# Three shared tiles instead of two in the score search of a sparse-attention block (Trainium2, one core)

## What is computed

```python
act = jax.nn.relu(jnp.einsum('bqhd,bsd->bqsh', qib, ki) * idx_scale)
score = jnp.einsum('bqsh,bqh->bqs', act, wib)
score = jnp.where(key_pos[None, None, :] < chunk_end[None, :, None], score, -jnp.inf)
_, sel = lax.top_k(score, topk)
```

## Time and profile before

| what | value |
|---|---|
| time, median of 3 runs | 1994.21 us (1988.74 to 1998.3) |
| time of the profiled execution | 1992.56 us |
| span of the profiled execution, first to last instruction | 1991.1 us |
| TensorE busy | 1716.8 us, 86% of the span |
| VectorE busy | 1114.5 us, 56% |
| ScalarE busy | 765.3 us, 38% |
| GpSimd busy | 379.1 us, 19% |
| mean granted TensorE clock | 0.945 of full speed |

### The profile page before, as it was taken

The page is one execution under the profiler, slowest core; times in us unless marked ns, Lnnn a source line. Parts: engine busy times, 40 slices in busy tenths (PEclk is TensorE's granted clock), DMA queues, the critical chain, the costliest instruction groups (busy, mean ns, idle before and its releaser), DMA issues. The chain is left out here.

```text
span 1991.1 us, 34351 instructions
## 1 busy us (share of the span) xinstructions
PE 1716.8 (86%) x14024; PEld 1387.2 (70%) x14024; DVE 1114.5 (56%) x2131; ACT 765.3 (38%) x1192; POOL 379.1 (19%) x337
## 2 busy tenths in 40 slices
PE   1999885699749967889769899999999999999796
PEld 0777663288637756778647688888888888888584
DVE  5266654789956644767535555444446544444463
ACT  4153432577445533333123333222233332223441
POOL 2232320032122210122313421000012100001442
PEclk9999987799969989999788899999999999999898
DMA  2116551122111023120072222222232332333122
GB/s 107 60 54 185 168 162 47 48 75 96 64 44 54 12 82 140 47 89 15 13 269 64 71 95 90 99 101 96 96 95 95 127 95 95 95 96 95 43 85 95
DMA packets 91959, 177.14 MB, mean 89 GB/s; under 512 B 7392, under 2 KB 51456, under 8 KB 91808
## 3 DMA queue, kind: packets, MB, share of 16 engines
q1 hardware_dynamic: 62688, 160.33, 24.1%
q10 hardware_dynamic: 29120, 14.68, 2.6%
HBM read 138.81 MB, written 36.18 MB: 88 GB/s over the span
## 5 line engine op out<-in xcount | busy, mean ns | idle before, releaser
L781 PE MATMUL acc<-h_hi,w_hi 128*128 128x512 f32 x768 | 309.3, 403 | 23.2 <-DVE w_lo L845 19.5
L782 PE MATMUL acc<-h_lo,w_hi 128*128 128x512 f32 x768 | 303.8, 396 | 0.0
L783 PE MATMUL acc<-h_hi,w_lo 128*128 128x512 f32 x768 | 303.4, 395 | 0.0
L685 ACT ACTIVATE w_hi<-w_raw 128x1024 fp32r<-128x1024 f32 x160 | 168.4, 1052 | 155.2 <-DMA w_raw<-w_ffn 144.3
L845 DVE TENSOR_TENSOR w_lo<-w_raw,w_hi 128x1024 fp32r<-128x1024 f32 x160 | 203.3, 1271 | 1.3 <-ACT w_hi L685 1.3
L781 PE MATMUL acc<-ffn_hi_lo,w_hi 128*128 128x512 f32 x512 | 200.2, 391 | 0.0
L782 PE MATMUL acc<-ffn_hi_lo,w_hi 128*128 128x512 f32 x512 | 199.3, 389 | 0.0
L783 PE MATMUL acc<-ffn_hi_lo,w_lo 128*128 128x512 f32 x512 | 199.3, 389 | 0.0
L781 PEld LDWEIGHTS acc<-h_hi,w_hi 128*128 128x128 f32 x768 | 147.2, 192 | 58.4 <-DVE w_lo L845 21.9
L504 POOL TENSOR_TENSOR post_squares_total<-post_squares_total,post_squares 128x512 f32<-128x512 f32 x42 | 64.6, 1539 | 570.9 <-ACT post_squares L497 570.1
L782 PEld LDWEIGHTS acc<-h_lo,w_hi 128*128 128x128 f32 x768 | 147.6, 192 | 32.2 <-issue 1.9
(11 more groups left out here) (304 smaller groups left out, 3587.7 us busy)
## 6 DMA issues: line engine op xcount, KB each, us to landing
w_raw<-w_ffn SPq DMA_DIRECT2D x128, 512.0 KB, 3.4
rwkv_factors<-factors_then_masks ACTq DMA_DIRECT2D x28, 512.0 KB, 6.3
factors<-rwkv_factors SPq DMA_DIRECT2D x32, 448.0 KB, 6.9
w_in_first_raw<-w_in SPq DMA_DIRECT2D x19, 512.0 KB, 3.8
w_raw<-w_out SPq DMA_DIRECT2D x16, 512.0 KB, 3.6
w_raw<-w_gate SPq DMA_DIRECT2D x16, 512.0 KB, 3.5
w_in_raw<-w_in SPq DMA_DIRECT2D x12, 512.0 KB, 3.9
x_in<-xT SPq DMA_DIRECT2D x8, 512.0 KB, 6.5
```

Of the source, the lines that this page charges most:

```text
L685: act.activation(wh[:, g % RING, :], w_raw[:, g % RING, :], ACT.Copy).then_inc(rounded, 1)
L781: pe.matmul(out, w_hi, a_hi, start=first, stop=False)
L782: pe.matmul(out, w_hi, a_lo, start=False, stop=False)
L783: return pe.matmul(out, w_lo, a_hi, start=False, stop=last)
```

## The change

`shared` gets a third tile, TILES - 3 = 5, which has 768 keys. ScalarE now counts tiles 5, 6 and 7 (768 + 896 + 1024 = 2688 keys a bit, before 1920), and VectorE tiles 2, 3 and 4 (384 + 512 + 640 = 1536 keys a bit, before 2304). The slice `both`, on which L1889 and the small instructions after the search work, covers three columns instead of two, as do the four small tiles of that part. VectorE waits for three counts of ScalarE a bit. The count of L1905 runs for three tiles instead of two.

```diff
         PER_BLOCK, BITS = 3, 32
-        shared = (TILES - 2, TILES - 1)
-        both = slice(shared[0] - FIRST, shared[1] - FIRST + 1)
+        shared = (TILES - 3, TILES - 2, TILES - 1)
+        both = slice(shared[0] - FIRST, shared[-1] - FIRST + 1)
         signs = {t: junk[t] for t in shared}
         limit, minus, reached = [ctx.sb(n, [P, T], F32) for n in ("limit", "minus_threshold", "reached")]
-        flip, low, high, carry = [ctx.sb(n, [P, 2], U32) for n in ("order_flip", "low_half", "high_half", "carry")]
+        flip, low, high, carry = [ctx.sb(n, [P, len(shared)], U32) for n in ("order_flip", "low_half", "high_half", "carry")]
...
                 link(last)
-                dve.wait_ge(counted, n * 2 + 2)
+                dve.wait_ge(counted, (n + 1) * len(shared))
                 link(dve.tensor_tensor(reached[:, :], count[:, :], limit[:, :], ALU.is_ge))
```

## The result

The changed kernel takes 2013.84 us in the median of 12 runs (2003.03 to 2021.65); the kernel before took 1996.49 us in the median of 12 runs beside it. The ratio is 1.0081, with a 95% interval of 1.0060 to 1.0102: slower by 0.8%. The profiled execution took 2009.5 us, with a span of 2008.0 us (1991.1 before) and a mean granted clock of 0.944.

The account below looks back on a forecast made before the run. VectorE's masks, starting where the search ends, end the stage; VectorE led the search, and ScalarE would lead after the change. Terms sum to +19.7 us: 2012.3 from the profiled execution, 2013.9 from the median; forecast 2013, range 2006 to 2021.

Parts of the forecast that it names:

- first block: Search's start up to ScalarE's copy of projection block 0: that copy comes 0.8 us later (0.4 to 1.1).
- copy 0 to copy 1: Between ScalarE's copies of projection blocks 0 and 1: 10.99 us becomes 13.10, so +2.11 us.
- copies 1 to 5, with values: ScalarE's copies of projection blocks 1 to 5, with turned values: each block 11.88 us becomes 14.01, +8.52 us together.
- Who leads: Search: a bit takes ScalarE 4.07 us, above VectorE's 3.81, so ScalarE leads in every bit.
- The price of the count: ScalarE's added count of 768 keys in each bit: 0.94 us, range 0.89 to 1.04.
- The way back: From ScalarE's last count through VectorE's comparison, predicated copies and new threshold to ScalarE's next start: 0.87 us a bit.
- The trip: ScalarE's copy and rounding for TensorE once a block: 1.85 us to the first count, 2.76 with turned values.
- The cover: Work costed at nothing: TensorE's projection gets gaps of 2 to 3 us a block but stays off the path.
- ScalarE's waits swallow the counts: Rival: ScalarE's idle time in the search absorbs the added counts, about 1990 us, not slower; chance 3%.
- The clock: Rival: new gaps make TensorE's clock fall, whole projection blocks at 1.2 GHz, near 2070 us; chance 3%.
- The stretch by GpSimd in the middle of the search: Rival: GpSimd's remainder stretches VectorE's return by 1.06 us in each of ten blocks, 2023 us; chance 4%.
- the change doesn't do what it says: Rival: for instance, the bound is a common one that neither tile assignment touches; no change, chance 2%.

Follow-up runs that it names:

- E1: The kernel before with a spare ScalarE count of 768 keys added in each bit, VectorE shedding nothing: 2011.72 us, ratio 1.0068.
- E5: The changed kernel with the smallest tile as the third, so ScalarE counts tiles 2, 6 and 7: ratio 1.0038 against the kernel before.
- E3: The changed kernel with ScalarE's third count over only 384 of the 768 keys: ratio 1.0028 against the kernel before.
- E2: The changed kernel with the third tile's count left out, so neither engine counts it: 1992.5 us, ratio 0.9986 against the kernel before.
- E4: The changed kernel with the copies of projection blocks 0 to 10 moved from ScalarE to VectorE: ratio 1.0032 against the kernel before.
- E6: The changed kernel with the copy of the best count run after the new threshold has gone out: ratio 1.0071 against the kernel before.
- E7: The kernel before with the copy of the best count run after the new threshold has gone out: ratio 0.9997.

## Why the prediction was right

The forecast was 2013 us in a range of 2006 to 2021, slower with 94%. Measured were 2013.84 us, slower with its whole interval. By its own steps, in the stage:

| term | forecast | measured |
|---|---|---|
| first block | +0.8 | 12.48 - 11.90 = +0.6 |
| copy 0 to copy 1 | +2.11 | 12.88 - 10.99 = +1.9 |
| copies 1 to 5, with values | +8.52 | 4 x (13.79 - 11.88) = +7.6 |
| copies 5 to 9 | +6.64 | 4 x (12.88 - 11.44) = +5.8 |
| copy 9 to the last comparison | +0.65 | 9.25 - 8.58 = +0.7 |
| L1905, third tile | +0.94 | +0.96 |
| together | +19.7 | +17.5 |

*Who leads.* Right: ScalarE leads in all 32 bits (the wait rows after), and E1 and E5 show that VectorE's share is worth nothing then.

*The price of the count.* Right: 0.932 us for 0.94. For 384 keys E3 measured 0.612, where the line through the two rows of before would have given 0.65 (0.94 less three times 0.097). An estimate by the rule of the Trainium skill, "ScalarE: Activation LUTs", section "What ACT_TABLE_LOAD costs", is 0.92 us for 768 keys; the trace lies between that and 0.94. The same estimate is 0.60 us for 384 keys, nearer to what E3 measured than the line is.

*The way back.* This is the term that was mis-sized. The forecast took 0.87 us from the earlier trace rows, where the bit follows the trip. There VectorE's comparison took 0.25 us instead of 0.17. In the changed kernel the way back has 0.79 us, outside the first block and the last bit. E2 has both in one block: 0.87 us before the bit at 477.43, the first after the rounding, and 0.79 before the one at 480.49. What ran beside the first of them on GpSimd:

```profile
474.48 2.41 POOL L380 TENSOR_TENSOR w_in_lo<-w_in_raw,w_in_hi 128x1024 fp32r<-128x1024 f32 x1 [8.46 <-ACT w_in_hi L376]
```

It ends at 476.89, and VectorE's comparison, from 476.66, took 0.25 us. Behind the first block this holds in all nine traces: the comparison takes 0.25 us or a little more where it begins while a remainder still runs, and 0.17 where none does. So the forecast's 0.87 us belongs to a bit that meets the remainder. The forecast had said itself that the remainder would no longer meet VectorE's small instructions, but it kept the price of a row in which it did. No run took the remainder away, so that it is the cause rests on this coincidence. A bit came out at 3.98 us instead of 4.07: about 0.1 us in each of the 18 inner bits of nine blocks is 1.6 to 1.8 of the 2.2 us between forecast and stage. The rest is 0.2 in the first block and 0.02 a block in the third bit's counts. The last bit's way back was 0.94 us although no remainder ran then; why, the runs don't show.

*The trip.* Right: 1.85 us without values and 2.76 with them, as in the earlier trace rows. A block without values grew by 1.44 us (12.88 - 11.44), and its two inner bits by only 0.17 each; the rest is the trip and the third bit's counts, which VectorE's counts no longer hide. E4 takes the copy out and gets 9.1 us back.

*The cover.* Right: TensorE's gaps came at block 6, and its last block was long done before the masks were. They were 1.7 to 2.2 us, for 2 to 3 forecast.

*The rivals.* That ScalarE's waits swallow the counts: E3 and E5 show that 0.61 us is already too much; the 0.39 us of the forecast was not tried. The clock: it stayed at the full level through all gaps. The stretch by GpSimd in the middle of the search: VectorE's comparison took 0.17 us in every bit but the second, where it took 0.59 beside GpSimd's work on `bias_rows`. That the change doesn't do what it says: the new shape stands 32 times in ScalarE's groups.

*The number.* That 2013 came within 1 us of 2013.84 is in part luck. The sum was 2.2 us too high, and the median that it was added to, 1994.21 of three runs, was 2.3 us below the 1996.49 of the twelve; the two errors cancel. The upper bound by the higher starting point is 1994.21 + 22.9 = 2017.1 and not 2016.8, which changes nothing in the range.

## What to carry to other kernels

Where two engines work through rounds that end in a common decision, the idle time of the one that follows is not room: subtract the way back of the round and the trips that it makes for others, and only the rest can take work. Here 0.67 us seemed free in one bit. Over a block it is less: in E3 a block without its three counts took 11.93 - 3 x 0.61 = 10.10 us, so 11.44 - 10.10 = 1.34 us was room for three, 0.45 each; with values it is 11.88 - (12.83 - 3 x 0.61) = 0.88, or 0.29 each. These are estimates, and only once VectorE has shed its count; no count that small was tried. What the leading engine sheds is worth nothing once the other leads, and work that had stood in its shadow comes onto the path with it. When a duration is taken from one row for a new arrangement, look whether something ran beside it there that won't run beside it any more.

## What the runs showed beyond this

The time outside the stage varies more from execution to execution than some of the edits change. From the last mask to the end it was 1432 to 1437 us in seven of the nine profiled executions, but 1445 in E6 and 1452 in E5, which change nothing there. The windows of the stage after the search show it, first of E5, then of the kernel before (busy us of PE, PEld, DVE, ACT, POOL, then the granted clock):

```profile
580.00:600.00 20.00, 18.69 (x74) 13.66 (x71) 5.18 (x22) 7.72 (x19) 3.20 (x5) 0.50 0.00 0
600.00:620.00 20.00, 18.62 (x95) 15.69 (x94) 9.63 (x41) 7.53 (x15) 4.32 (x6) 0.60 0.00 1
```

```profile
580.00:600.00 20.00, 17.49 (x135) 14.34 (x136) 11.28 (x52) 11.06 (x25) 5.82 (x9) 1.00 0.00 1
600.00:620.00 20.00, 18.70 (x139) 14.61 (x139) 12.42 (x52) 12.41 (x25) 5.15 (x8) 1.00 0.15 54
```

In E5 TensorE is busy for 18.7 of 20 us at a granted clock of 0.50, and of 0.60 in the next window, that is mostly at 1.2 GHz, and gets 169 matmuls done in 40 us. The kernel before is at 2.4 GHz in both and gets 274 done. Two marks tell what this cost. From the last mask to ScalarE's second scaling of queries (L2060 of the kernel before) it was 17.1 to 17.4 us in all nine executions. To its third it was 57.1 to 57.9 us in seven of them, but 70.7 in E5 and 64.9 in E6, where the granted clock was 0.50 from 590 to 610 us too. So this one stretch took about 13 us more in E5 and 7 in E6, the larger part of what lies outside the stage. TensorE had been idle just before for 34.1 us in E5 and 34.9 in E6, but also for 35.2 in the changed kernel, where the clock was back at 1.00 from 600 us on; so the length of the pause doesn't tell them apart. What does stays open.

That it is a matter of the execution and not of the edit is borne out by the other runs: the profiled execution of E5 was the slowest of its 12 (2017.09 us, the median 2004.49) and had the lowest mean granted clock (0.932, the others 0.938 to 0.945), and that of E6 was the slowest of its 8. A single span would have told of a loss of 24.5 us in E5 where the stage has 7.4. Distances inside the stage are steadier: the search of the changed kernel and of E1 agreed within 0.1 us, those of the kernel before and of E7 too, and those of E3 and E5 within 0.3.
